# First-block scores issued in pairs, top-k rounds spread over the units, a shorter inverse-root chain and high parts first in a two-block transformer kernel

## What is computed

```python
def first_block(x, ...):
    for l in range(2):
        h = x @ w_in[l]
        o_a = sliding_window_sink_attn(rope(a_q), rope(a_k), a_v, sinks)   # 8 heads, 2 key heads, window 128
        o_b = indexer_sparse_attn(rope(b_q), rope(b_k), b_v, ...)          # 4 heads; each row keeps its 128 best keys
        o_c = mla_attn(...)                                               # 4 heads, 96 wide, causal
        x = layer_norm(ALPHA * x + concat(o_a, o_b, o_c) @ w_out[l])
        x = layer_norm(ALPHA * x + moe_ffn(x, ...))
    return x

def second_block(h, ...):
    for layer in range(2):
        h = h + 0.5 * rms(swiglu(rms(h)))             # ffn0, ffn2
        h = h + rms(mixer(rms(h)))                    # pool, dilated
        h = h + 0.5 * rms(swiglu(rms(h)))             # ffn1, ffn3
    return h
# rms(v) = v * rsqrt(mean(v*v) + eps) * gain ; layer_norm likewise, with the mean taken out
```

## Time and profile before

| | us |
|---|---|
| median of three runs | 3485.66 |
| the profiled execution's own time | 3482.8 |
| its span, first to last instruction | 3481.0 |
| PE busy | 3267.5 (94%) |
| DVE busy | 1936.0 (56%) |
| ACT busy | 1387.3 (40%) |
| chain of waits: PE / DVE / DMA | 68% / 13% / 9% |
| mean granted clock of TensorE | 0.976 |

### The profile page before, as it was taken

How to read it: one execution, slowest core, us unless ns; L and a number is a source line. 1 busy time by engine, 2 the same in 40 slices (tenths; PEclk the granted TensorE clock), 3 DMA queues, 4 the chain that set the end, 5 groups by cost and what they waited for, 6 DMA issues and landing times.

```text
span 3481.0 us, 42214 instructions
## 1 busy us (share of the span) xinstructions
PE 3267.5 (94%) x14912; PEld 2560.7 (74%) x14912; DVE 1936.0 (56%) x3022; ACT 1387.3 (40%) x2048; POOL 394.8 (11%) x241
## 2 busy tenths in 40 slices
PE   8899898898998899999998999999999899899998
PEld 6667777765677777788866788877888667678886
DVE  5764677567646874654455643546353643565343
ACT  4453576444535674322222322233222554532121
POOL 3101122321011223000010100010000100010000
PEclk9999999999999999999998999999999999999999
DMA  3101699421015995132312232324232312023232
GB/s 120 51 1 61 204 318 314 165 62 48 1 61 186 320 318 190 58 101 91 99 58 68 78 98 89 99 70 145 91 96 97 127 55 68 30 73 99 88 101 74
DMA packets 174980, 389.60 MB, mean 112 GB/s; under 512 B 11312, under 2 KB 70064, under 8 KB 174192
## 3 DMA queue, kind: packets, MB, share of 16 engines
q1 hardware_dynamic: 173424, 377.45, 33.4%
q0 software_dynamic: 1408, 10.23, 0.8%
HBM read 381.34 MB, written 6.29 MB: 111 GB/s over the span
## 4 chain that ended last, share of the span: by engine, by line
PE 68%; DVE 13%; DMA 9%; ACT 4%; DVEq 2%; issue 2%; POOL 1%; POOLq 0%; ACTq 0%; SPq 0%
PE ps L562 19%; PE ps L564 18%; PE ps L563 18%; DMA gate_up_stage<-in_w_gu 8%; DVE moe_lo L1957 4%; ACT moe_hi L1150 2%; PE ps L679 2%; PE ps L734 2%; PE ps L712 2%; PE ps L840 1%; ACT w_hi L1150 1%; PE ps L670 1%; PE ps L775 1%; PE ps L793 1%; PE ps L784 1%
## 5 line engine op out<-in xcount | busy, mean ns | idle before, releaser
L1581 DVE TENSOR_TENSOR w_lo<-w_stage,w_hi 128x1024 fp32r<-128x1024 f32 (+3 forms) x310 | 398.5, 1287 | 845.6 <-ACT w_hi L1150 844.9
L562 PE MATMUL ps<-xs_hi,w_hi 128*128 128x512 f32 (+2 forms) x1952 | 775.3, 397 | 50.1 <-DVE w_lo L1581 14.7
L1150 ACT ACTIVATE w_hi<-w_stage 128x1024 fp32r<-128x1024 f32 (+3 forms) x350 | 382.0, 1093 | 1018.5 <-PE ps L564 1005.8
L564 PE MATMUL ps<-xs_hi,w_lo 128*128 128x512 f32 (+2 forms) x1952 | 769.6, 394 | 0.0
L563 PE MATMUL ps<-xs_lo,w_hi 128*128 128x512 f32 (+2 forms) x1952 | 769.3, 394 | 0.0
L562 PEld LDWEIGHTS ps<-xs_hi,w_hi 128*128 128x128 f32 (+2 forms) x1952 | 367.2, 188 | 151.4 <-issue 27.8
L564 PEld LDWEIGHTS ps<-xs_hi,w_lo 128*128 128x128 f32 (+2 forms) x1952 | 367.6, 188 | 85.0
L563 PEld LDWEIGHTS ps<-xs_lo,w_hi 128*128 128x128 f32 (+2 forms) x1952 | 368.1, 189 | 82.6
L1957 DVE TENSOR_TENSOR moe_lo<-gate_up_stage,moe_hi 128x1024 fp32r<-128x1024 f32 x224 | 268.2, 1239 | 120.4 <-ACT moe_hi L1150 119.9
L1150 ACT ACTIVATE moe_hi<-gate_up_stage 128x1024 fp32r<-128x1024 f32 x224 | 226.7, 1055 | 142.5 <-DMA gate_up_stage<-in_w_gu 134.3
L564 PE MATMUL ps<-h_hi,w_lo 128*128 128x512 f32 x704 | 278.1, 395 | 0.0
(11 more groups left out here) (366 smaller groups left out, 4903.9 us busy)
## 6 DMA issues: line engine op xcount, KB each, us to landing
gate_up_stage<-in_w_gu SPq DMA_DIRECT2D x112, 1024.0 KB, 5.6
w_stage<-in_f_gu SPq DMA_DIRECT2D x174, 512.0 KB, 3.5
down_stage<-in_w_dn SPq DMA_DIRECT2D x112, 512.0 KB, 5.8
w_stage<-in_f_dn SPq DMA_DIRECT2D x64, 704.0 KB, 4.0
w_stage<-in_w_in SPq DMA_DIRECT2D x30, 512.0 KB, 3.6
w_stage<-in_d_qk SPq DMA_DIRECT2D x24, 512.0 KB, 3.6
w_stage<-in_w_out SPq DMA_DIRECT2D x16, 512.0 KB, 3.6
w_stage<-in_d_v SPq DMA_DIRECT2D x12, 512.0 KB, 3.6
```

Of the source, the lines that this page charges most:

```text
L562: pe.matmul(o, lh, rh, start=start, stop=False)
L564: return pe.matmul(o, ll, rh, start=False, stop=stop)
L1150: copy = lambda o, i: nc.scalar.activation(o, i, ACT.Copy)
L1581: tt(w_lo[:, s, 0:n], stage[:, s, 0:n], w_hi[:, s, 0:n].bitcast(F32), ALU.subtract).then_inc(w_split, 1)
```

## The change

Four things, in one kernel.

1. `attend` on PE: scores of n + 4 and n + 5 are issued together at every even n, with four banks in place of three; the filler of one pass stands before the transposes of every unit from 1 to 47; rows are turned one step earlier, into the batch's own bank 6 or 7, and the high and low parts follow one step earlier. The first mix of a batch now waits for the low part (`ot_split`) of the batch two ahead where it waited for its rows.
2. `attend` on DVE: the 28 rounds of a layer stand at 14 steps of the window units, 8 of the 96-wide units and 6 of the sparse units (24, 4 and 0 before). The marks of blocks 1 and 2 become a mask at step 47, those of block 3 at step 57.
3. `norm_columns`: 8 short instructions in place of 11 (12 where the result was halved: the half is now in the gains, four small instructions once).
4. `first_tile`: for tile 0 the high-part matmuls of all outputs come first and wait for the high part alone, then the low-part matmuls. The fillers around a norm shrink: three to one before the spread, five to two and a half behind it (to three behind the second layer norm).

```diff
-        S_BANKS, S_RING = (2, 3, 1), 4
+        S_BANKS, S_RING = (0, 1, 2, 3), 4
...
+            def first_tile(fill, outs):
+
+                pe.wait_ge(xs_hi_done, 8 * fill + 1)
+                for o, hi, lo in outs:
+                    pe.matmul(o, hi, xs_hi[:, 0, :], start=True, stop=False)
+                    pe.matmul(o, lo, xs_hi[:, 0, :], start=False, stop=False)
+                pe.wait_ge(xs_ready, 8 * fill + 1)
+                for o, hi, _ in outs:
+                    pe.matmul(o, hi, xs_lo[:, 0, :], start=False, stop=False)
...
                         if un["B"] >= 2:
-                            pe.wait_ge(rows_ready, l * BATCHES + un["B"] - 1)
+                            pe.wait_ge(ot_split, l * BATCHES + un["B"] - 1)
...
-                    if B > 0:
-                        pe.wait_ge(ot_split, l * BATCHES + B)
                     for i in range(nt):
-                        last = pe.transpose(ps[:, 0, i * P:i * P + P], rows_o[:, B % 2, i * P:i * P + P], ident[:, :])
+                        last = pe.transpose(ps[:, 6 + B % 2, i * P:i * P + P], rows_o[:, B % 2, i * P:i * P + P], ident[:, :])
...
-                for n in range(3):
+                for n in range(4):
                     scores(UN[n], n, S_BANKS)
                 keep_clock(4, 4)
                 for n in range(N + 5):
                     if n < N:
-                        if n > 0 and BA[UN[n]["B"]]["sinks"]:
+                        if 0 < n < 48:
                             keep_clock(1, 4 + n % 2, 1)
...
-                    if n + 3 < N:
-                        pe.wait_ge(masked, c0 + n + 1)
-                        scores(UN[n + 3], n + 3, S_BANKS)
+                    if n % 2 == 0 and n + 4 < N:
+                        pe.wait_ge(masked, c0 + n + 2)
+                        for i in (n + 4, n + 5):
+                            scores(UN[i], i, S_BANKS)
                     if 0 <= n - 1 < N:
                         mix(n - 1)
-                    if n - 4 in LAST:
-                        turn_rows(LAST.index(n - 4))
+                    if n - 3 in LAST:
+                        turn_rows(LAST.index(n - 3))
...
-                keep_clock(3)
+                keep_clock(1)
                 spread(NORM[name + "_out"], [RB])
-                keep_clock(5 if n < 3 else 0)
+                if n < 3:
+                    keep_clock(2)
+                    keep_clock(1, 7, 2)
...
-                ts(t.bitcast(I32), var.bitcast(I32), 1, None, ALU.logical_shift_right)
-                v.drain()
-                ts(r.bitcast(I32), t.bitcast(I32), -1.0, float(0x5F3759DF), ALU.mult, ALU.add)
-                v.drain()
-                for _ in range(3):
-                    stt(t, r, -0.5, r, ALU.mult, ALU.mult)
-                    v.drain()
-                    tt(t, t, var, ALU.mult)
-                    v.drain()
-                    stt(r, t, 1.5, r, ALU.add, ALU.mult)
-                    v.drain()
-                if half:
-                    ts(r, r, 0.5, None, ALU.mult)
+                ts(r.bitcast(I32), var.bitcast(I32), -0.5, float(0x5F3759DF), ALU.mult, ALU.add)
+                v.drain()
+                tt(t, r, r, ALU.mult)
+                v.drain()
+                tt(t, t, var, ALU.mult)
...
-                ROUND_UNITS = ([n for n in range(32) if n % 4 < 3] + list(range(32, 48, 2)))[:len(rounds)]
+                ROUND_UNITS = [n for n in range(32) if n % 16 in (0, 2, 4, 6, 8, 10, 12)] + list(range(32, 48, 2)) + [48, 50, 52, 53, 54, 56]
```

More of the change, by code:

```diff
@@ L576, in first_pair @@
                         meanwhile()
+                    if k == 0:
+                        first_tile(fill, [(ps[:, banks[s], :], w_hi[:, s, 0:P], w_lo[:, s, 0:P]) for s in range(2)])
+                        continue
                     pe.wait_ge(xs_ready, 8 * fill + k + 1)
@@ L592, in first_four @@
                         meanwhile()
+                    if k == 0:
+                        first_tile(fill, [(ps[0:M, FOUR_BANKS[q], :], FOUR_HI[q][:, 0:M], FOUR_LO[q][:, 0:M])
+                                          for q, M in enumerate((P, P, P, M3))])
+                        continue
                     pe.wait_ge(xs_ready, 8 * fill + k + 1)
@@ L1238, in attend @@
                         copy(probt[:, n % 2, 0:W], ps[:, 4 + n % 2, 0:W]).then_inc(pt_copied, 1)
-                    if n - 5 in LAST:
-                        B = LAST.index(n - 5)
+                    if n - 4 in LAST:
+                        B = LAST.index(n - 4)
                         ba = BA[B]
@@ L1586, in split_first, with norm_columns @@
                 tt(FOUR_LO[q][:, 0:n], stage[:, q % 2, 0:n], FOUR_HI[q][:, 0:n].bitcast(F32), ALU.subtract).then_inc(w_split, 1)
-            def norm_columns(n, kind, n0, half=False):
+            def norm_columns(n, kind, n0):
                 if kind == "c":
@@ L1708, in attend, with causal_top @@
                 c0, N = l * UNITS, len(UN)
-                ROUND_UNITS = ([n for n in range(32) if n % 4 < 3] + list(range(32, 48, 2)))[:len(rounds)]
+                ROUND_UNITS = [n for n in range(32) if n % 16 in (0, 2, 4, 6, 8, 10, 12)] + list(range(32, 48, 2)) + [48, 50, 52, 53, 54, 56]
+                assert len(ROUND_UNITS) == len(rounds)
+                def causal_top(qt):
+                    work = maskb[:, qt, 0:(qt + 1) * P]
+                    ts(work, work, TAKEN * 0.99, MASKED, ALU.is_gt, ALU.mult)
                 def mask_scores(n):
@@ L1764, in attend @@
                         top_round(rounds[ROUND_UNITS.index(n)])
-                    elif n == ROUND_UNITS[-1] + 1:
+                    elif n == 47:
                         v.drain()
-                        for qt in range(1, NT):
-                            work = maskb[:, qt, 0:(qt + 1) * P]
-                            ts(work, work, TAKEN * 0.99, MASKED, ALU.is_gt, ALU.mult)
+                        causal_top(1)
+                        causal_top(2)
                         v.drain()
-                    if n - 7 in LAST:
-                        low(LAST.index(n - 7))
+                    elif n == 57:
+                        v.drain()
+                        causal_top(3)
+                        v.drain()
+                    if n - 6 in LAST:
+                        low(LAST.index(n - 6))
             def attend_wide(U, c0, hi_of, lo_of):
@@ L2043, in _ @@
             tt(wr_lo[:, :], wr[:, :], wr_hi[:, :].bitcast(F32), ALU.subtract).then_inc(wr_ready, 1)
+            for name in ("ffn0_out", "ffn1_out", "ffn2_out", "ffn3_out"):
+                ts(ngain[:, GAIN[name], :], ngain[:, GAIN[name], :], 0.5, None, ALU.mult)
             for l in range(L):
@@ L2152, in statistics, with residual @@
                 v.drain()
-            def residual(name, t, half, after):
-                norm(NORM[name], "rms", SQ[name], half, (lambda: rest_of_first(after)) if after else None)
+            def residual(name, t, after):
+                norm(NORM[name], "rms", SQ[name], (lambda: rest_of_first(after)) if after else None)
                 def scaled(m):
@@ L2240, in dense @@
                     v.drain().then_inc(place_free, 1)
-                residual(name + "_out", y, True, after)
+                residual(name + "_out", y, after)
             def angles():
```

29 lines of the change are left out of this document (19 added, 10 removed).

## The result

The kernel after takes 3442.59 us (median of four runs, 3436.81 to 3443.66), the kernel before beside it 3487.27: a ratio of 0.9866, with a 95% interval of 0.9847 to 0.9884, or 44.7 us. The forecast was 35 us less and 3450, within 3436 to 3473. The profiled execution of the kernel after took 3443.66 us, 39 less than that of the kernel before.

A forecast was written before the change was run, and what follows sets the result against it. PE, busy for 94% of the span, was taken as the bound. From the profiled 3482.8 us, 21 came off for two attention layers and 14 for norms, giving 3447.8; the median lies 2.9 above, so 3450, range 3436 to 3473.

The forecast's parts named there:

- Window units: Attention's window units: paired scores on different partition halves overlap, PE stays the bound narrowly; minus 9 us a layer.
- First and last units: Attention's ends: the stretch ahead of the window units minus 2 us a layer, the last stretch minus 1.5.
- 96-wide units: Attention's 96-wide units: pairs can't overlap, fillers cost 4.3 us, clock may repay 3.4; sum 0, between -2 and +2.5.
- Sparse units: Attention's sparse units: six rounds make DVE the bound at 16.7 us; plus 1 a layer, between +0.5 and +1.8.
- Norms: All norms: shorter DVE chain, high parts first and fewer fillers; together minus 14 us, bounds -6 to -18.
- First-block norms: Six norms of the first block: the shorter chain counts where PE has nothing else; 3 us less.
- The second block: Norms ahead of pooling and dilated 1.4 us less, behind six parts 12 less, with 2 taken off for the clock.
- Rival 1: Attention: evacuation (DVE) becomes the bound or pairing gives less; about 3466, span 3459 to 3475; chance 0.22.
- Rival 2: Norms: the clock falls at the twelve that lose fillers, 25 us back; 3475, no change to be told; chance 0.10.
- Rival 3: Attention: the new low-part wait stops PE at each batch of four, 16 waits; slower, about 3502; chance 0.06.

The follow-up runs named there:

- e7: Kernel before with rows turned into the batch's own bank, high and low parts one step earlier, first mix waiting for the low part; ratio 1.0026.
- e12: Kernel before with e7's own bank, plus the freed bank as fourth score bank, scores issued one at a time; run once, 3458.9 us beside 3481.0.
- e1: Kernel before with the norms' part alone (shorter chain, high parts first, fewer fillers), attention as before; 3469.5 us against 3483.4, ratio 0.9960.
- e4: Kernel after with the old fillers around the norms (three ahead of the spread, five behind it); ratio 0.9880.
- e10: Kernel after with no fillers among the 96-wide units, one a unit among the sparse ones, old fillers around the norms; 3432.9 us, ratio 0.9858.
- e11: e10 with the low part ahead of the round and two sparse-unit rounds moved to window units 14 and 30; 3431.5 us, ratio 0.9842.
- e3: Kernel after with scores issued one at a time in place of pairs, all else as it is; ratio 0.9988.
- e8: Kernel after with rounds placed as before (24 window, 4 96-wide, none sparse) and all blocks' marks masked at step 39; 3453.3 us against 3481.7, ratio 0.9920.
- e9: Kernel after with DVE's low part ahead of the round (or block 3's mask) in steps that have both; ratio 0.9869.
- e5: Kernel after without its 16 fillers among the 96-wide units; ratio 0.9877.
- e6: Kernel after with a filler in front of the transposes of the sparse units too; ratio 0.9867.
- e2: Kernel before with the attention part alone (paired scores, own banks for turned rows, rounds spread), norms as before; 3452.3 us, ratio 0.9910.

## Why the prediction came out as it did

- **Window units: right mechanism, a little too small.** Overlap of the halves, DVE with fewer rounds and PE as the bound are what the trace shows. I put a pair at 2.75 and a batch at 11.5; a pair takes 2.61, since the mix that lost its score is shorter too. The 12.2 a layer of the table against 9 makes the miss look larger than it is: the forecast took the 43.46 us of the earlier trace rows for 24 units, and by the masks they are 25 (the 43.04 of layer 1 are 24). Three whole batches went from 42.6 to 32.5 us in layer 0 and to 32.1 in layer 1, 10.0 and 10.4 against 9; the batches are 10.7, 10.1 and 11.7 us long in layer 0.
- **First and last units:** 5.9 and 3.3 against 4 and 3. In the first the sum was luck: the stretch that I priced (units 3 to 9) gave 0.9 and 0.6 us where I had 2 a layer, and units 0 to 3, which I had not priced, gave 2.2 in each layer.
- **96-wide units: wrong step.** I summed PE and DVE as if one of them were full, and let the clock repay the fillers. Neither was full (26.27 and 18.01 of 28.25); the bank shared with the turned rows (e7, where the clock rose too) and the three banks for scores (e12) made it longer. Both are in the diff, and I gave neither a term.
- **Sparse units: right that DVE's rounds decide, 4.9 against 2.** DVE's work is 15.1 (16.7 forecast), with 1.3 us of waits at the start. Layer 0 gave 1.5, near the forecast 1; layer 1 gave 3.4, and there DVE also waits 1.6 us for scores at half clock. PE was forecast to wait for masks there; it waits 0.3 us for them and 2.7 for the low part.
- **Norms: total right, places wrong.** Alone they gave 14 (e1), as forecast. First-block norms gave more: the way from layer 0's second layer norm to the next norm's spread is 2.6 shorter than before in the kernel after with three fillers, and 0.8 to 2.1 in e4, e10 and e11 with five, so that the fillers' share is open. The rest of the 9.2 was not taken apart. The second block gave 4.2 in this profile. With the same norms it gave about 4.4 in e3, e8 and e9 and 7.4 to 8.2 in e1, e5 and e6; with the old fillers 8.0 in e4 and 5.2 in e10 and e11. The clock falls at other norms in each, but other parts of the block shift too: it is 2.7 us longer in e2, which has it unchanged. The term was 11.4, with only 2 taken off for the clock; at pooling alone it took 1.8.
- **Rivals.** Rival 1 did not come in the window units, but its mechanism, DVE as the bound, is true of the sparse ones; e8 shows the window units with it. Rival 2's mechanism is there at single norms and in the sparse units, not at its price: the mean granted clock went from 0.976 to 0.972, at most 14 us over the span, and e4, with 0.979, took no other time. Rival 3's wait is there once a layer in the sparse units (2.7 us) and once in the 96-wide ones (0.5), not at each batch of four; it costs nothing in layer 0, and together with the half clock perhaps part of the 1.6 us in layer 1.

So the total was near by luck, by errors of opposite sign in the profile: some 12 us more from the attention and 5 more from the first block's norms, 7 less from the second block's.

By the page "TensorEngine Tiling (Array Packing)" of the Trainium skill, section "PSUM Bottleneck", packing may leave the copies out of PSUM as the bottleneck. e8 agrees in part: with pairs and DVE's old rounds, 43.09 us with DVE at 39.34. DVE is the engine that takes the scores out of PSUM, but what fills it there are the rounds. By the page "TensorE: Matmul & The Clock Gate" of the Trainium skill, section "Why this matters for your kernels", idle gaps between bursts are to be avoided. The sparse units agree (0.77 with gaps, 1.00 with a filler a unit, e6); e3's 31.64 us at 0.51 with PE busy do not.

## What to carry to other kernels

Where two engines are both within a tenth of a stretch's length, cost a change of either by the other's sum, and make both changes or none: here each alone gave 2.7 and 0.4 us and both 12.2. Where neither engine is full, look at the number of buffers between them too: here a fourth bank gave 1.6 and 2.7 us in a stretch of 27. But look first whether the idle time is waiting or the gaps between dependent steps, as on DVE in the sparse units. Take fillers out one place at a time with the granted clock beside it, and in more than one profile: sixteen of them cost 1.25 us and held nothing, and at the norm behind pooling the clock fell with the old number in five kernels of seven.

## What was not expected of the hardware

**The same program part differs by 16 us between profiles.** From the first layer norm's spread to the second's, which no kernel here changed but for the norms, with the weights of the experts streaming in: in e12 (layer 0) and e1 (layer 1):

```profile
311.15:686.31 375.16, 342.23 (x1516) 268.27 (x1514) 264.54 (x323) 227.36 (x290) 94.68 (x40) 0.97 0.68 232
```

```profile
1004.73:1396.28 391.55, 345.59 (x1516) 270.28 (x1514) 258.42 (x321) 228.23 (x290) 96.54 (x40) 0.96 0.68 226
```

The matmuls are as many, PE's busy time is 3 us longer, and the rate from memory is 232 against 226 GB/s. What makes the difference stays open. A difference of 10 us between two single profiles of this kernel can lie in there alone.

**The clock may stay at half under a busy PE** for over 30 us (e3); the longest stretch at half clock in the trace of the kernel after lasts 14 us.
